# High and low halves of stick-breaking values and of transposed weights: splitting them before the value matmuls, and transposing q and k whole

## What is computed

```python
xn = rmsnorm(x, norm_g)
gq, gk, gv, gate, alr, sq, sk, sv = split(xn @ w_in)          # 1024 -> 3088 columns
log_a = log_sigmoid(alr @ w_a2 + b_a2) / 16
o_gla = gla(gq * 64**-0.5, gk, gv, log_a)                     # 4 heads, chunks of 64 frames
q, k = rmsnorm(sq, q_g), rmsnorm(sk, k_g)                     # 8 heads of 64
# stick-breaking attention, strictly causal; k and v include 512 cached frames for the sample
z = q @ k.T / 8
l = where(mask, log_sigmoid(-z), 0)
w = where(mask, exp(log_sigmoid(z) + reverse_cumsum(l) - l), 0)
o_sb = w @ v
h = x + concat(rmsnorm(o_gla, g) * silu(gate), o_sb) @ w_out
y = h + square(relu(rmsnorm(h, g2) @ w_up)) @ w_down
```

## Time and profile before

| | |
|---|---|
| time, median of 3 runs | 3234.82 us (3234.36 to 3235.14) |
| profiled execution, its own time | 3235.57 us |
| its span, first to last instruction | 3233.5 us |
| mean granted TensorE clock | 0.979 |
| busy share of the span | PE 96%, PEld 83%, DVE 59%, ACT 54%, POOL 34% |
| phase_front | 0 to 863 us |
| attention of block 0, alone | 876 to 926 us |
| dense work with attention | 926 to 2932 us |
| dense work of the last block | 2932 to 3233 us |

### The profile page before, as it was taken

How to read it: one execution, slowest core, us unless ns; L and a number is a source line. 1 busy time by engine, 2 the same in 40 slices (tenths; PEclk the granted TensorE clock), 3 DMA queues, 4 the chain that set the end, 5 groups by cost and what they waited for, 6 DMA issues and landing times. The chain is left out here.

```text
span 3233.5 us, 49170 instructions
## 1 busy us (share of the span) xinstructions
PE 3104.9 (96%) x18410; PEld 2669.8 (83%) x18410; DVE 1905.3 (59%) x3388; ACT 1732.7 (54%) x3224; POOL 1102.1 (34%) x642
## 2 busy tenths in 40 slices
PE   6999999999769998999999999999999999999999
PEld 5778787877669998888888988888898888888998
DVE  2565656556446665666666777776756676653333
ACT  3544534444357764655555666666646555543443
POOL 0231414214135662333223322222332332334665
PEclk9999999999869999999999999999999999999999
DMA  4554544444364554232333422222252333334443
GB/s 149 176 165 146 181 131 146 154 130 126 116 183 139 175 166 154 72 101 85 111 94 119 126 80 87 87 89 89 88 179 84 107 98 110 96 98 140 130 134 117
DMA packets 309565, 400.69 MB, mean 124 GB/s; under 512 B 69249, under 2 KB 223890, under 8 KB 308306
## 3 DMA queue, kind: packets, MB, share of 16 engines
q1 hardware_dynamic: 309330, 397.55, 39.2%
HBM read 339.95 MB, written 57.54 MB: 123 GB/s over the span
## 5 line engine op out<-in xcount | busy, mean ns | idle before, releaser
L1847 POOL TENSOR_TENSOR st_ul<-st_ur,st_uh 128x1024 fp32r<-128x1024 f32 x180 | 430.5, 2413 | 766.1 <-ACT st_uh L1655 766.1
L1854 POOL TENSOR_TENSOR st_dl<-st_dr,st_dh 128x1024 fp32r<-128x1024 f32 x180 | 427.5, 2397 | 686.3 <-ACT st_dh L1665 686.3
L1821 DVE TENSOR_TENSOR st_ya<-st_ya,st_dp 128x512 f32<-128x512 f32 x544 | 368.7, 680 | 102.0 <-PE st_dp L1575 100.5
L1622 ACT ACTIVATE st_a<-st_z 128x512 f32<-128x512 f32 (+3 forms) x336 | 177.0, 527 | 395.9 <-PE st_z L1434 261.6
L1747 DVE TENSOR_TENSOR_SCAN st_g<-st_z,st_g,st_a 128x511 f32<-128x511 f32 (+3 forms) x336 | 370.9, 1104 | 16.0 <-DVE st_g L1740 0.8
L1808 DVE TENSOR_TENSOR st_tl<-st_dp,st_th 128x512 fp32r<-128x512 f32 (+2 forms) x168 | 96.8, 576 | 440.7 <-ACT st_dp L1703 440.6
L1457 PEld LDWEIGHTS st_po<-st_v,st_wt 128*128 128x128 f32 x2256 | 303.6, 195 | 41.2 <-DMA st_v<-out_new_v 19.0
L1575 PE MATMUL st_dp<-st_dh,st_tl 128*128 128x512 f32 x1020 | 336.7, 401 | 0.0
L1575 PE MATMUL st_dp<-st_dh,st_th 128*128 128x512 f32 x1020 | 336.0, 401 | 0.6 <-DVE st_ya L1821 0.6
L1575 PE MATMUL st_dp<-st_dl,st_th 128*128 128x512 f32 x1020 | 335.2, 400 | 0.0
L492 PE MATMUL fr_pj<-fr_wl,fr_xh 128*128 128x512 f32 x816 | 329.9, 404 | 0.0
(11 more groups left out here) (166 smaller groups left out, 5845.2 us busy)
## 6 DMA issues: line engine op xcount, KB each, us to landing
st_ur<-in_w_up SPq DMA_DIRECT2D x75, 1024.0 KB, 5.4
st_dr<-in_w_down SPq DMA_DIRECT2D x75, 1024.0 KB, 4.9
fr_wr<-in_w_in SPq DMA_DIRECT2D x96, 512.0 KB, 4.0
k_t<-fr_stT SPq DMA_DIRECT2D x21, 512.0 KB, 4.2
st_ur<-in_w_out SPq DMA_DIRECT2D x10, 1024.0 KB, 5.7
st_dr<-in_w_out SPq DMA_DIRECT2D x10, 1024.0 KB, 6.2
fr_xb<-in_x SPq DMA_DIRECT2D x17, 512.0 KB, 5.0
q_t<-fr_stT SPq DMA_DIRECT2D x17, 512.0 KB, 4.9
```

What stands on the lines that cost most here:

```text
L1821: dve.tensor_tensor(part, part, dp[:, k % BANKS], ALU.add).then_inc(s_fd, 1)
L1847: pool.tensor_tensor(ul[:, c], ur[:, c], raw(uh[:, c]), ALU.subtract).then_inc(s_ul, 1)
L1854: pool.tensor_tensor(dl[:, k], dr[:, k], raw(dh[:, k]), ALU.subtract).then_inc(s_dl, 1)
```

## The change

- Front: q and k items are transposed before they are split. PE makes four transposes of `nq` into one bank (was eight into two), in the plan at the slot's end + 8200 (was + 11000), behind POOL's gain alone. ACT then copies the bank to `sth` (high) and DVE subtracts to `stl` (low). The store is four DMAs of 64 partitions each (was one). The bank is freed by DVE.
- Front: values are split too. For each SB_V slot ACT copies the bank a second time into `vst`, DVE writes the low half beside it, and SP stores 512 KB to a new scratch tensor `v_s`. Four tiles of cached v (`"w"` items) go the same way.
- Stream: `v` is loaded from `v_s` (high and low, 128 columns per head). The weights' transposes are split: ACT copies `tp` to `wth` in part 1, ahead of `weights`; DVE subtracts to `wtl` in part 1, behind `negated_softplus` (was a copy in part 0). Each key tile has two fp32r matmuls: `wth` x (v high, v low), 128 columns, and `wtl` x v high, 64 columns.
- Stream: a finished output tile is copied from its second 64 columns by ACT (`output_low`) and DVE adds the first 64 (`output`, part 2, ahead of the scan).

```diff
@@ class Front
-            tt += [Use(self.item_at(s) + 11000 + a, ("t", self.item[s], 0, a), "A") for a in range(2)]
+            if s[0] != "w":
+                tt.append(Use(self.item_at(s) + 8200, ("t", self.item[s], 0, 0), "D"))
@@ phase_front, SP
-                    yield plan.tt.at("t", c, 0, 1) + 2500
-                    sp.dma_start(dst.rearrange("h p k -> p h k"), raw(stT[:, c % 2])).then_inc(s_sd[c % 2], 16)
+                    yield plan.tt.at("t", c, 0, 0) + 2600
+                    dst = dst.rearrange("(a e) (i p) k -> e i p a k", e=2, i=2)
+                    for e in range(2):
+                        for i, part in enumerate((sth, stl)):
+                            sp.dma_start(dst[e, i], raw(part[64 * e:64 * e + 64, item_buffer(c)])).then_inc(s_sd[item_buffer(c)], 16)
+            def split_value_stores():
+                    sp.dma_start(vs[at:at + P], raw(vst[:, k % 2])).then_inc(s_vd[k % 2], 16)
@@ phase_front, PE
-                        pe.wait_ge(s_ql, b + 1)
+                            pe.wait_ge(s_qg, b - NI + 1)
                         for h in range(4):
-                            mm = pe.transpose(bank[:, h * P:(h + 1) * P], raw(stk[:, b % 2, 4 * a + h]).rearrange("p a d -> p (a d)"), idt[:])
+                            mm = pe.transpose(bank[:, h * P:(h + 1) * P], nq[:, b % 2, h * P:(h + 1) * P], idt[:])
@@ phase_front, ACT
+                            act.activation(vst[:, k % 2, :, 0, :], bank.rearrange("p (h d) -> p h d", d=HD), ACT.Copy).then_inc(s_vh, 1)
-                    act.activation(stk[:, c % 2, :, 0, :], nq[:, c % 2].rearrange("p (h d) -> p h d", d=HD), ACT.Copy).then_inc(s_qh, 1)
-                        act.activation(stT[:, c % 2, 4 * a:4 * a + 4, :],
+                    act.activation(sth[:, n % 2], tt[:, plan.tt.bank("t", c, 0, 0)].rearrange("p (h k) -> p h k", k=P), ACT.Copy).then_inc(s_qh, 1)
@@ phase_front, DVE
-                    yield plan.item_at(s) + 7600
+                    yield plan.tt.at("t", c, 0, 0) + 1700
+                    dve.tensor_tensor(stl[:, n % 2], tt[:, ...], raw(sth[:, n % 2]), ALU.subtract).then_inc(s_ttd, 1)
+            def value_rests():
+                    dve.tensor_tensor(vst[:, k % 2, :, 1, :], src.rearrange("p (h d) -> p h d", d=HD), raw(vst[:, k % 2, :, 0, :]),
+                                      ALU.subtract).then_inc(done, 1)
@@ phase_stream, PE
-                    mm = pe.matmul(po[:, tt % 2 * HD:(tt % 2 + 1) * HD], wt[:, u % 3, c * P:(c + 1) * P],
+                    pe.matmul(out, wth[:, u % 3, c * P:(c + 1) * P], tile.rearrange("p i d -> p (i d)"), start=(un.first and c == 0), stop=False)
+                    mm = pe.matmul(out[:, 0:HD], wtl[:, u % 3, c * P:(c + 1) * P], tile[:, 0], start=False, stop=(un.last and c == un.n - 1))
@@ phase_stream, ACT
+            def transposed_high(u):
+                act.wait_ge(s_tr, u + 1)
+                act.activation(wth[:, u % 3, 0:n], tp[:, 0:n], ACT.Copy).then_inc(s_wh, 1)
             def part1(u):
+                if u(2) is not None:
+                    transposed_high(u(2))
                 if u(1) is not None:
                     weights(u(1))
@@ phase_stream, DVE
-                dve.tensor_copy(wt[:, u % 3, 0:n], tp[:, 0:n]).then_inc(s_wt, 1)
+                dve.wait_ge(s_wh, u + 1)
+                dve.tensor_tensor(wtl[:, u % 3, 0:n], tp[:, 0:n], raw(wth[:, u % 3, 0:n]), ALU.subtract).then_inc(s_wt, 1)
+                    dve.tensor_tensor(dst, dst, po[:, tt % 2, 0:HD], ALU.add).then_inc(s_of, 1)
```

More of the change, by code:

```diff
@@ L318, in kept_done, with item_buffer, consumed @@
             eng.wait_ge(s_ngd[q % 2], 16 * (q // 2 + 1))
+        columns = [c for c, s in enumerate(plan.items) if s[0] != "w"]
+        def item_buffer(c):
+            return columns.index(c) % 2
+        def consumed(eng, c):
+            if plan.items[c][0] == "w":
+                eng.wait_ge(s_vl, plan.items[c][1] + 1)
+            else:
+                eng.wait_ge(s_tt, plan.tt.full("t", c, 0, 0))
         def x_at(t):
@@ L836, in item_sums @@
             def item_sums():
-                for s in plan.items[NC:]:
-                    r = plan.item[s] - NC
+                for s in plan.items[NI:]:
+                    r = plan.item[s] - NI
                     yield plan.end(*s) + 800
```

200 lines of the change are left out of this document (120 added, 80 removed).

## The result

The changed kernel takes 3337.82 us (median of 4 runs, 3335.06 to 3342.07), the kernel before 3234.59 us beside it: ratio 1.032, 95% interval 1.0303 to 1.0338, 103 us slower. The forecast was 3235.2 us, no difference, with a range of 3217 to 3258. The profiled execution took 3338.72 us with a span of 3336.9 us.

The account below looks back on a forecast made before the run. PE was taken to bound front and stream. Terms +2 - 16.6 - 4 + 13 + 3 + 3 = +0.4 on the profiled 3235.6 us gave 3236.0, as a median 3235.2: no difference, range 3217 to 3258.

Parts of the forecast that it names:

- What bounds the kernel: Front and stream: PE, busy 811 of 829 and 1961 of 2000 us; only its pace and waits count.
- The value matmuls: Stream: 2256 short matmuls keep costing about a new stationary tile each, 0.111 us before; +2 us, bounds -4 to +5.
- Rival 3: Stream: value matmuls run at the pace of their columns, 153 us fewer, 3084 us; chance 0.03.
- The transposes of the front: Front: 38 items lose four of eight transposes, 152 x 0.109 us off PE's path; -16.6 us.
- their old waits: Front: of 8.1 us that the old transposes stood waiting, 4 us go; bounds 0 and 8.
- The new wait of the front: Front: transposes, half a slot earlier, wait for POOL's gain at eight late items; +13 us, bounds 0 and +18.
- ACT in the front: Front: ACT loses copies and gains 21 copies of values at 0.6 us, all covered; 0 us.
- DVE in the stream: Stream: DVE's copy becomes an equally long subtraction that waits for ACT, mostly covered; +3 us, bounds 0 and +32.
- Rival 2: Stream: ACT's copy becomes late and DVE's next dense sum waits behind it; +32 us, 3264 us; chance 0.22.
- Rival 1: Front: DVE scales the items early enough, so no new wait; -13.6 us, 3221 us; chance 0.25.
- Attention of block 0: Attention of block 0: ACT, busiest there, has 5.3 us more copies, partly hidden; +3 us, bounds 0 and +6.
- What would show it: Signs: front's end within 5 us, 13 us idle before its transposes, value records at 0.11 us, no new stream idle.

Follow-up runs that it names:

- e10: e6 without the second matmul of each value pair (low weights times high values, 64 columns): 3133.5 us.
- e7: Changed kernel with the values' part undone and the q and k transposes at their old place in the slot: 3213.2 us.
- e3: Changed kernel with the front's q and k transposes back at their old place in the slot (+11000): 3315.9 us.
- e4: Changed kernel with the values' part undone in front and stream, only q, k and cached keys transposed whole: 3232.2 us.
- e5: Changed kernel with the loads of cached values in a list of their own, asked for earlier: 3322.0 us.
- e1: Changed kernel with ACT's high copy at the end of part 0 and DVE's low half ahead of the negated softplus: 3276.4 us.
- e15: Changed kernel, orders untouched, DVE's one-column difference reading the running sum as scalar operand instead of a second SBUF tensor: 3281.7 us.
- e12: Changed kernel with two PSUM banks for the stream's transposes and three instead of four for dense work: 3305.4 us.
- e13: Changed kernel with one PSUM bank for the stream's transposes and three instead of four for dense work: 3355.7 us.
- e9: Changed kernel with only ACT's high copy moved to the end of part 0, DVE's low half left in place: 3341.2 us.
- e14: Changed kernel with DVE's low half between its negated softplus and the one-column difference: 3281.1 us.
- e6: Changed kernel with the edits of e1, e3 and e5 together: 3238.1 us.
- e17: e6 with the scalar-operand edit of e15: 3231.7 us.
- e11: e6 with ACT's high copy one step earlier still, ahead of its softplus: 3244.1 us.
- e16: e7 with the scalar-operand edit of e15: 3210.8 us.

## Why the prediction was wrong, step by step

- **What bounds the kernel: right.** What was lost is time in which PE waits, and time at the lower clock level around such waits. The second had no term in the sum: some 15 us in the stream and 18 in the front, by the estimate above.
- **The value matmuls, +2 us (-4 to +5): right.** Eight records in the kernel after, read as in the earlier trace rows:

```profile
2025.48 0.22 PE L1512 MATMUL st_po<-st_v,st_wth 128*128 128x128 f32 x1
...
2026.28 0.47 PE L1629 MATMUL st_dp<-st_dh,st_th 128*128 128x512 f32 x1
2026.60 0.63 PE L1629 MATMUL st_dp<-st_dl,st_th 128*128 128x512 f32 x2
```

  2026.60 - 2025.48 - 0.23 = 0.89 us for eight, 0.111 each, the same as before to the digit. Rival 3 is out; e10 says the same. (Its sum was off by little: 3235.2 - 2 - 153 is 3080, not 3084.)
- **The transposes of the front, -16.6, and their old waits, -4: right.** e7 has both and no new wait: 21.5 us less against 20.6. PE's idle time in the front fell by 4.3 us; the 3.2 us for the low half of x stayed.
- **The new wait of the front, +13 (0 to +18): right in its mechanism, place and cause, undersized.** 19.0 us in six waits, where 13 were forecast; taking them away was worth 21.9 us in e3 and 19.0 from e4 to e7. The forecast priced a wait at its length and left out the clock behind it. Taken with the two terms above, the columns' part alone was forecast at -7.6 us and measured at about -2 (e4).
- **ACT in the front, 0: wrong.** The term "gains 21 copies of values at 0.6 us", held to be covered, counted ACT's busy time and not what these copies wait for. Four of them need a load that one list issues in order behind another load, whose buffer PE frees late. SP's and the cache's loads were priced by issue time alone. Price: 16 us (e5).
- **DVE in the stream: wrong, and most of the miss.** The step that failed is "Late next would be `wtl`: PE needs it a full slot (about 5 us) after the transposes". For its own values, yes. But the transposes of the next unit wait for the same step (`pe.wait_ge(s_wt, u)`), because there is one bank; they stand a third of a slot ahead of those values, and the low half itself had moved a third of a slot back. The forecast looked for who waits for VectorE's dense sums and for the values, and did not follow the bank. It also took the low half at its 0.69 us, where what counted was what now stands ahead of it on VectorE: a wait for ACT's softplus, and the one-column difference, 149.5 us busy in 200 operations already in the kernel before. That row was in the profile and was not asked why it takes 747 ns. The term was +3; the rest of the span grew by 77 us, of which the order of the steps is worth 61 (e1), the block by POOL 56 (e15) and the bank 50 (e12 against e13), all for the same chain.
- **Rival 2 (slower, 3264)** had the right side and the wrong engine. ACT's copy is late, as it said, but an earlier copy alone gained nothing (e9), and e14 and e15 won 56 us with that copy where it was. Its mechanism, DVE's dense sums behind the low half, did not occur: PE's waits have no such row. Its price of 32 us was for that.
- **Rival 1 (the items come in time)** fell with the six waits for POOL's gain.
- **Attention of block 0, +3 (0 to +6): right,** 65.1 - 63.6 = 1.5 us.
- **What would show it** did its work: "the front should end within 5 us of where it did" failed: it ended 26 us later; "PE should show no new idle time" named the values and the sums, where there is none, and not the transposes, where there is.

What is left open: e6 and e17 keep 8 to 11 us in the rest of the span over the kernel before. Nine waits of PE before the transposes, 9.8 us, stand against 4.7 us of the same place in e4, and neither ACT's place (e11) nor VectorE's block (e17) removed them. All of PE's idle time behind block 0's attention is 52.3 us in e6, against 44.6 before.

## What to carry to other kernels

When a copy out of PSUM is made by two engines in turn, ask not when its result is needed but when its bank is, and read what each of the two engines has in its queue ahead of that step, with the idle time and the odd long instruction in it. An operation whose time is out of proportion to its size (one column, 747 ns) is a wait in disguise: here a scalar operand in place of a second tensor took 56 us off the changed kernel, and nothing that can be told off the versions in which nothing that PE needed stood behind it. And a list of loads that is issued in order is as late as its latest buffer, so loads with different buffers belong in lists of their own. And a wait that a change opens on PE is not paid by its length alone: read the granted clock behind it too.

## What the runs showed of the hardware

- VectorE's one-column difference of two tensors in SBUF stood still while POOL subtracted one tensor in SBUF from another: 0.16 us when free, over 0.6 us (1.9 in the median, 2.4 at most) in 69 of the 200, every one of them released some 0.02 us after POOL's subtraction. With one tensor and a scalar the mean fell from 728 to 214 ns.
- Taking that block away moved the whole kernel by 1.7%, since a bank of PSUM hung on it, and by nothing measurable where none did (e16).
- A store of 64 partitions by 4 x 512 B took SP 0.62 us to issue, one of 128 partitions 0.42 us; 114 more of the former cost the front nothing that can be seen.
- Around a wait of PE of 5.6 us the granted clock was 0.77 over 15 us, and around one of 6.86 us it was 0.50 over 10 us, with dense matmuls 0.43 us apart instead of 0.23. Over the last part of the span 56.8 us more of idle time came with 31.1 us more at the lower level.
